# A decoder layer with 32 experts: the order in which the weight queue brings gate/up and down weights

## What is computed

```python
h = xb @ w_gu[e] + b_gu[e]               # 1024 -> 2048
g = jnp.minimum(h[:, 0::2], SWIGLU_LIMIT)
up = jnp.clip(h[:, 1::2], -SWIGLU_LIMIT, SWIGLU_LIMIT)
act = (up + 1.0) * (g * jax.nn.sigmoid(SWIGLU_ALPHA * g))
return act @ w_dn[e] + b_dn[e]           # 1024 -> 1024
```

## Time and profile before

| | us |
|---|---|
| Median of 3 runs | 1151.42 (1150.93 to 1152.32) |
| The profiled execution | 1153.59 |
| Its span | 1151.7 |
| TensorE busy in the span | 1069.7 |
| VectorE busy | 335.8 |
| ScalarE busy | 140.0 |

### The profile page before, as it was taken

One profiled execution on the slowest core, in us unless ns is written; L12 is line 12 of the kernel. 1 busy time (PEld: TensorE's weight loads), 2 busy tenths in 40 slices (PEclk: granted clock), 3 DMA queues, 4 the chain that ended last, 5 costly groups with the idle time before them and its releaser, 6 DMA issues.

```text
span 1151.7 us, 14763 instructions
## 1 busy us (share of the span) xinstructions
PE 1069.7 (93%) x5498; PEld 439.4 (38%) x5498; DVE 335.8 (29%) x728; ACT 140.0 (12%) x264; POOL 20.5 (2%) x45
## 2 busy tenths in 40 slices
PE   3978888999999999999999899999998999999997
PEld 2866344333333333333333333333333333333332
DVE  2386448321212122222222212122121212121213
ACT  2227221000000000000000000000000000000000
POOL 5000000000000000000000000000000000000000
PEclk9998896999999998999999999999999999999999
DMA  8923217999999999999999999999999999999991
GB/s 254 377 100 69 99 48 291 405 417 418 418 420 418 420 418 420 418 418 418 419 417 419 417 419 417 420 417 420 416 420 417 419 419 418 420 418 420 415 415 53
DMA packets 83021, 422.10 MB, mean 367 GB/s; under 512 B 7458, under 2 KB 14906, under 8 KB 50215
## 3 DMA queue, kind: packets, MB, share of 16 engines
q1 hardware_dynamic: 81326, 418.25, 89.7%
q0 software_dynamic: 1232, 2.73, 0.8%
q10 hardware_dynamic: 440, 0.83, 0.2%
HBM read 420.46 MB, written 2.33 MB: 367 GB/s over the span
## 4 chain that ended last, share of the span: by engine, by line
PE 60%; DMA 22%; SPq 8%; DVE 4%; ACT 3%; issue 2%; DVEq 0%; ACTq 0%
PE ps L1451 22%; DMA ring<-in_w_gate_up_dram 20%; PE ps L1492 14%; SPq L273 8%; PE ps L1414 5%; PE ps L1378 4%; PE ps L1140 3%; PE ps L1273 3%; DMA regA<-in_w_in_dram 2%; PE ps L1460 2%; PE ps L1114 2%; PE ps L1389 1%; PE ps L1383 1%; ACT regA L608 1%; PE ps L1422 1%
## 5 line engine op out<-in xcount | busy, mean ns | idle before, releaser
L1451 PE MATMUL ps<-ring,regA 128*64 128x512 f32 x2048 | 461.2, 600 | 24.3 <-DMA ring<-in_w_gate_up_dram 22.4
L1451 PEld LDWEIGHTS ps<-ring,regA 128*64 128x64 f32 x2048 | 145.0, 138 | 334.5 <-issue 259.4
L1060 DVE TENSOR_SCALAR regA<-ps 128x512 f32<-128x512 f32 x32 | 22.1, 692 | 427.1 <-PE ps L1460 427.1
L617 ACT ACTIVATE regA<-regA 128x512 f32<-128x512 f32 x32 | 20.1, 630 | 798.9 <-DVE regA L1060 798.9
L1492 PE MATMUL ps<-ring,regA 128*64 128x512 f32 x512 | 113.4, 595 | 0.0
L1077 DVE COPY regA<-ps 64x512 f32<-64x512 f32 x62 | 42.7, 689 | 222.0 <-PE ps L1492 221.0
L1378 PE MATMUL ps<-regA 128*64 128x256 f32 x512 | 64.1, 393 | 0.0
L1045 DVE TENSOR_TENSOR x_row<-x_row,ps 128x512 f32<-128x512 f32 x72 | 46.1, 684 | 58.8 <-PE ps L1414 58.1
L1492 PEld LDWEIGHTS ps<-ring,regA 128*64 128x64 f32 x512 | 36.4, 137 | 65.8 <-issue 65.6
L1414 PE MATMUL ps<-regA 128*128 128x512 f32 (+1 forms) x136 | 59.7, 594 | 1.1 <-DVE regA L1074 1.1
L1140 PE MATMUL ps<-hT_t,regA 128*128 128x264 f32 x224 | 53.5, 399 | 3.7 <-DMA regA<-in_w_in_dram 3.7
(11 more groups left out here) (270 smaller groups left out, 635.8 us busy)
## 6 DMA issues: line engine op xcount, KB each, us to landing
ring<-in_w_gate_up_dram SPq DMA_DIRECT2D x256, 1024.0 KB, 20.7
ring<-in_w_down_dram SPq DMA_DIRECT2D x64, 1024.0 KB, 22.5
regA<-in_w_down_dram SPq DMA_DIRECT2D x16, 1024.0 KB, 19.4
regC<-in_w_down_dram SPq DMA_DIRECT2D x16, 1024.0 KB, 20.2
regD<-in_w_down_dram SPq DMA_DIRECT2D x16, 1024.0 KB, 21.0
hT_t<-in_w_down_dram SPq DMA_DIRECT2D x16, 1024.0 KB, 21.8
regA<-in_w_in_dram SPq DMA_DIRECT2D x7, 1024.0 KB, 12.1
regA<-in_w_out_dram SPq DMA_DIRECT2D x2, 1024.0 KB, 9.8
```

Source lines behind the costliest of these rows:

```text
L1451: mm = pe.matmul(ps[64 * h:64 * h + 64, 1 + n, :], xT[:, kt % 4, 64 * (kt // 4):64 * (kt // 4) + 64], ring[:, kt, 1024 * h + 512 * n:1024 ...
```

## The change

SP's order stays as it is up to gu(10), dn(11). Then gu(11), gu(12) and dn(12) follow, and from there on an expert's down weights stand behind its own gate/up weights: gu(13), dn(13), ... gu(28), dn(28), gu(29), dn(29). The end is gu(30), gu(31), dn(30), dn(31). The conditions in `load_gu` and `load_dn` are the same.

```diff
+E_TURN = 5
...
-            with sp.Fori(0, E // 2 - 2) as p:
+            with sp.Fori(0, E_TURN) as p:
                 load_gu(p * 2 + 1, p * 2 + 1)
                 load_dn(p * 2 + 2, p * 2 + 2, False)
                 load_gu(p * 2 + 2, p * 2 + 2)
                 load_dn(p * 2 + 3, p * 2 + 3, True)
+            load_gu(2 * E_TURN + 1, 2 * E_TURN + 1)
+            load_gu(2 * E_TURN + 2, 2 * E_TURN + 2)
+            load_dn(2 * E_TURN + 2, 2 * E_TURN + 2, False)
+            with sp.Fori(E_TURN + 1, E // 2 - 2) as p:
+                load_gu(p * 2 + 1, p * 2 + 1)
+                load_dn(p * 2 + 1, p * 2 + 1, True)
+                load_gu(p * 2 + 2, p * 2 + 2)
+                load_dn(p * 2 + 2, p * 2 + 2, False)
             load_gu(E - 3, E - 3)
-            load_dn(E - 2, E - 2, False)
+            load_dn(E - 3, E - 3, True)
             load_gu(E - 2, E - 2)
             load_gu(E - 1, E - 1)
+            load_dn(E - 2, E - 2, False)
             load_dn(E - 1, E - 1, True)
```

TensorE and VectorE run the last two items in another order. The loops over pairs end one pair earlier, item 29 is written out, and `item` is split into functions (`gate_up`, `act_transposes`, `down` on TensorE; `swiglu`, `y_copy` on VectorE) of which the last two items are put together, first TensorE's part, then VectorE's:

```diff
+            def last_two():
+                gate_up(E - 2, True, E // 2)
+                pe.wait_ge(m_idx, E - 1)
+                gather(E - 1, whole)
+                pe.wait_ge(m_act, E - 1)
+                act_transposes()
+                x_transposes(E - 1)
+                gate_up(E - 1, False, E // 2)
+                down(E - 2, True, E // 2)
+                pe.wait_ge(m_act, E)
+                act_transposes()
+                pe.wait_ge(m_idx, E)
+                place(E - 2, beside_last)
+                down(E - 1, False, E // 2)
+                pe.wait_ge(m_add, (N_PLACED - 2) * ADDS + ADDS)
```

```diff
+            def last_two():
+                dve.wait_ge(m_xg, E - 1)
+                choose_rows(E - 1)
+                choose_gates(E - 1)
+                swiglu(E - 2)
+                place_gates(E - 2, upper)
+                dve.wait_ge(m_gated, E - 1)
+                slots_of(E - 1, whole)
+                swiglu(E - 1)
+                dve.wait_ge(m_used, SLOTS * (E - 1) + KT)
+                y_copy(E - 2, upper)
+                add(N_PLACED - 2, beside_last)
+                place_gates(E - 1, whole)
+                dve.wait_ge(m_used, SLOTS * E)
+                y_copy(E - 1, whole)
+                dve.wait_ge(m_gated, E)
+                dve.wait_ge(m_add, (N_PLACED - 2) * ADDS + ADDS)
```

More of the change, by code:

```diff
@@ L1052, in item @@
             def item(q, ahead, r, n_placed):
-                gu = ps[:, 1:3, :].rearrange("p n c -> p (n c)")
                 if ahead:
@@ L1058, in item, with swiglu @@
                     choose_gates(q + 1)
+                swiglu(q)
+                if n_placed is not None:
+                    add(n_placed, beside_ahead if ahead else beside_last)
+                place_gates(q, r)
+                dve.wait_ge(m_used, SLOTS * q + SLOTS)
+                y_copy(q, r)
+                dve.wait_ge(m_gated, q + 1)
+                if ahead:
+                    slots_of(q + 1, upper if r == lower else whole)
+                if n_placed is not None:
+                    dve.wait_ge(m_add, n_placed * ADDS + ADDS)
+            def swiglu(q):
+                gu = ps[:, 1:3, :].rearrange("p n c -> p (n c)")
                 dve.wait_ge(m_gu, q + 1)
@@ L1068, in item, with y_copy @@
                 dve.tensor_tensor(act_sb, up_sb, sig_sb, ALU.mult).then_inc(m_act, 1)
[L1069 to L1072, removed]
+            def y_copy(q, r):
                 if r == whole:
@@ L1077, in item @@
                         dve.tensor_copy(y_sb[n][r, :], ps[64 * n:64 * n + 64, 4, :]).then_inc(m_ysb, 1)
[L1078 to L1083, removed]
             slots_of(0, upper)
@@ L1095, in _ @@
             dve.wait_ge(m_add, ADDS * half + ADDS)
-            with dve.Fori(half, E // 2 - 1) as p:
+            with dve.Fori(half, E // 2 - 2) as p:
                 item(p * 2 + 1, True, lower, p + 1)
                 item(p * 2 + 2, True, upper, None)
-            item(E - 1, False, whole, N_PLACED - 2)
+            item(E - 3, True, lower, N_PLACED - 3)
+            def last_two():
[15 more added lines that the diff above has]
+                dve.wait_ge(m_add, (N_PLACED - 2) * ADDS + ADDS)
+            last_two()
             n_over = dve.value_load(ovi[0:1, 0:1], min_val=0, max_val=N_OVER)
@@ L1440, in place_biases, with item, transposes_copied, gate_up @@
                 mm.then_inc(m_pl, 1)
-            def item(q, ahead, even, n_placed, alone, n_loads):
+            def item(q, ahead, even, n_placed, n_loads):
+                gate_up(q, even, n_loads)
+                if ahead:
+                    pe.wait_ge(m_idx, q + 1)
+                    gather(q + 1, whole if even else upper)
+                pe.wait_ge(m_act, q + 1)
+                act_transposes()
+                def transposes_copied():
+                    pe.wait_ge(m_aT, q + 1)
+                    pe.wait_ge(m_xT, q + 2)
+                if ahead:
+                    x_transposes(q + 1)
+                    if n_placed is not None:
+                        place(q - 1, beside_ahead, False, transposes_copied)
+                down(q, even, n_loads)
+                if n_placed is not None:
+                    pe.wait_ge(m_add, n_placed * ADDS + ADDS)
+            def gate_up(q, even, n_loads):
                 pe.wait_ge(m_xT, q + 1)
@@ L1463, in item, with act_transposes @@
                 mm.then_inc(m_gu, 1)
[L1464 to L1471, removed]
+            def act_transposes():
                 for j in range(4):
@@ L1474, in item, with down @@
                 mm.then_inc(m_atr, 1)
[L1476 to L1483, removed]
+            def down(q, even, n_loads):
                 pe.wait_ge(m_aT, q + 1)
@@ L1495, in item @@
                     mm.then_inc(m_used, 1)
-                if n_placed is not None:
-                    pe.wait_ge(m_add, n_placed * ADDS + ADDS)
             pe.wait_ge(s_xns, 16 * 3)
@@ L1507, in pairs @@
                 with pe.Fori(p0, p1) as p:
-                    item(p * 2 + 1, True, False, p + biases if biases else p, False, p + 1)
-                    item(p * 2 + 2, True, True, None, False, p + 2)
+                    item(p * 2 + 1, True, False, p + biases if biases else p, p + 1)
+                    item(p * 2 + 2, True, True, None, p + 2)
             pe.wait_ge(s_zero, 10)
             half = (E_BIAS - 1) // 2
-            item(0, True, True, None, False, 1)
+            item(0, True, True, None, 1)
             pairs(0, half, 0)
@@ L1516, in _ @@
             pe.wait_ge(m_add, ADDS * half + ADDS)
-            pairs(half, E // 2 - 1, 1)
-            item(E - 1, False, False, N_PLACED - 2, False, E // 2)
+            pairs(half, E // 2 - 2, 1)
+            item(E - 3, True, False, N_PLACED - 3, E // 2 - 1)
+            def last_two():
[8 more added lines that the diff above has]
+                pe.wait_ge(m_act, E)
+                act_transposes()
+                pe.wait_ge(m_idx, E)
+                place(E - 2, beside_last)
+                down(E - 1, False, E // 2)
+                pe.wait_ge(m_add, (N_PLACED - 2) * ADDS + ADDS)
+            last_two()
             pe.wait_ge(S["ovd"], 1)
@@ L1525, in _ @@
                     x_transposes(m + E)
-                    item(m + E, False, True, m + (N_PLACED - 1), True, m + (E // 2 + 1))
+                    gate_up(m + E, True, m + (E // 2 + 1))
+                    pe.wait_ge(m_idx, m + (E + 1))
+                    place(m + (E - 1), beside_last, True, lambda: pe.wait_ge(m_act, m + (E + 1)))
+                    pe.wait_ge(m_act, m + (E + 1))
+                    act_transposes()
+                    down(m + E, True, m + (E // 2 + 1))
+                    pe.wait_ge(m_add, (m + (N_PLACED - 1)) * ADDS + ADDS)
             place(n_over + (E - 1), beside_last, True)
```

## The result

The changed kernel takes 1145.97 us (median of 5 runs, 1145.39 to 1147.4) against 1151.42 for the kernel before (5 runs, 1150.93 to 1153.17): the medians lie 5.4 us apart. The ratio of the runs is 0.9944, 95% interval 0.9932 to 0.9956; of 1151.42 us that is 6.4 us, by the interval 5.1 to 7.8. The sum had said 7.2 us and 1144.2. Its medians lie 7.8 us apart.

The account below looks back on a forecast made before the run. The weight queue was taken to set the pace from expert 13, TensorE's remaining work the end; gate/ups landing 10.35 us earlier bring down(31) from 1142.85 to 1135.6, so 1151.42 − 7.2 = 1144.2 us, range 1140.8 to 1149.0.

Parts of the forecast that it names:

- The sum: Whole kernel: down(31) ends at 1135.6 in place of 1142.85, 7.2 us off the median 1151.42, giving 1144.2 us; chance 0.68.
- The pace: Expert loop from expert 13: the weight queue sets the pace at 60.70 us a pair; TensorE needs 56.68.
- T: End of the weight queue: the landing of the last weights, dn31[3], forecast to stay at 1130.5 us.
- four downs' worth of time: Queue from gu(12) on: every gate/up slot lands four down slots, 10.35 us, earlier, gu29[7] at 1060.2.
- The turn: Queue where its order switches, gu(12) and gu(13): 7.5 and 7.6 us of work still queued at issue, so no loss.
- Both dry-queue rivals: Queue empties: once at the turn, 4.8 us later, 1149.0 (chance 0.08); or again and again, 1158.6 (chance 0.06).
- After the turn: Experts 13 to 19: TensorE, at most 10.5 us behind, is back on the queue's pace by expert 19.
- the rate of 4 us a pair: Expert loop: TensorE's spare time per two experts, 60.70 − 56.68, with which it catches up with earlier landings.
- The rival that saw no effect: After the turn: TensorE stays behind and reads gu(29) at 1070.55 as before; 1152.8 us; chance 0.06.
- The tail: Last experts: gu(30) from 1078.5, gu(31) from 1098.8, place(30) from 1124.2, down(31) to 1135.6, then 8.85 us of unchanged code.
- the difference taken from the median: Final sum: the 7.2 us is subtracted from the runs' median 1151.42, not the profiled 1153.59, giving 1144.2.
- The clock: Rival in the tail: the granted clock falls as down(30) waits slot by slot and place(30) for a copy; chance 0.10.

Follow-up runs that it names:

- c2: Changed kernel's queue with dn(30) back ahead of gu(31), TensorE and VectorE running the old program; ratio 0.9933 to the kernel before.
- c3: Kernel before with only the order of the last two experts on TensorE and VectorE changed, queue order as before; ratio 1.0026, 3.0 us slower.
- d2: Changed kernel with the queue's turn at the very start (E_TURN = 0, first loop taken out); ratio 0.9983 to the kernel before, 2.0 us faster.
- c4: Changed kernel with the queue's turn at gu(27) instead of gu(11); ratio 0.9976 to the kernel before, 2.8 us faster.
- d4: Changed kernel with the queue's turn at gu(21) (E_TURN = 10); ratio 0.9938 to the kernel before.
- c1: The changed kernel timed again without edit, in a second set on one chip; ratio 0.9938 to the kernel before, 7.1 us of 1152.03.
- d3: Changed kernel without placing and adding experts 29 and 30 (results missing), expert 31's down in PSUM bank 2; ratio 0.9902 to the kernel before.

## Why the prediction was right

**The pace and T.** "If the last landing stays at T = 1130.5": it landed at 1129.8, with the front 0.14 us earlier. That four downs' worth of time, 10.35 us, moves from ahead of the gate/ups to behind them held for gu29[7] (1060.2 forecast, 1059.71 measured). With the tail's old order c2 gives the same gain, and with the queue's old order c3 gives none: the earlier landings are the cause.

**The turn.** The backlog of 7.5 and 7.6 us that I had worked out from landings was 7.3 and 7.4, and cost nothing. Both dry-queue rivals rested mainly on these two numbers, and d2 shows that the mechanism is real and what it costs with less. Their price of 4.8 us a restart is no constant: by GB/s the first spell in d2 cost (112 + 133) / 418 × 10 = 5.9 us, near the 3.5 us in which nothing was queued plus the 4.7 − 2.49 = 2.2 by which a landing from an empty queue takes longer than a step of a full one. In the second, with 3.2 us queued, 1.3 us of transfers were missing.

**After the turn.** TensorE was to be back on the queue's pace by expert 19: gu(18) still runs through without a wait at 714.89 and gu19[7] waits for its landing at 754.07. c4 and d4 test the rate of 4 us a pair on which this rests. The rival that saw no effect, with TensorE staying behind, is what c4 shows in part.

**The tail**, forecast and profile: gu(30) from 1078.5, 1078.08; gu(31) from 1098.8, 1098.24; dn30[3]'s read from 1120.7, 1119.99; place(30) from 1124.2, 1123.48; down(31) to 1135.6, 1134.76. Every step came 0.4 to 0.8 us early; T itself was 0.7 early.

**The size.** The step that the first set put in doubt was the difference taken from the median: 1144.2 against 1145.97. The term itself, down(31) ending 7.2 us earlier, measured 8.1 between two profiles whose fronts are 0.14 us apart; c1 gave 7.1 by its ratio and 7.8 by its medians, and both intervals hold 7.2. In the first set the two longest of the five runs of the changed kernel (1147.11 and 1147.4) show a mean granted clock of 0.974, the other three 0.977 or 0.978; without their traces, where they lost time stays open.

**The clock.** I put this rival in the wrong place. In down(30)'s waits and before place(30) the clock stayed at 1.00. It fell to 0.50 at the start of gu(31), in the profiles of c1, c3, c4, d2, d3 and d4 (not in the first one), where `last_two` lets TensorE wait for the copy of expert 31's inputs, and there it cost 1.9 us. In c3 and c4 this went straight into the time. In c1 it went into the wait for dn30[3]: gu(31) took 15.47 us and down(31) still ended 75.13 us after gu29[7]'s read. A fall like the one at gu(9) of the kernel before, where the clock stood at 0.58 ahead of 16.88 us of gate/up against the usual 13.73, would have cost 3.15 us. That waits between the last matmuls bring the clock down is not borne out for down(30): its waits of some 0.6 us a slot (0.9 in the forecast) left it at 1.00.

**What I had not seen:** half of the change brings nothing that these runs can tell. The prediction costed the queue and the new tail together and never asked what the old tail would do behind the new queue. c2 answers it: the same time within the intervals, with a dozen lines of SP's program and nothing else.

Whether a tail could reach d3's floor with all its work was not tried. In front of down(31) stand 1.0 us of TensorE's wait for the copies of expert 30's results (they end at 1121.97 + 1.41 = 1123.38, place(30) starts at 1123.48) and 4.2 of place(30); without them, part of that time would be waits for the last slots, so that 3 us of it are to be had at most, about the scatter of these runs.

## What to carry to other kernels

Where a queue that is always full feeds an engine with little time to spare, the order of the queue does not change when the last byte lands as long as the queue stays full (here 1129.8 against 1130.5), but it decides how much work is left then: bring last what has the least work behind it, here down weights. An engine that lags needs about as many rounds as lead divided by gain per round (10.35 / 4, so three; one gave a part of the gain) to use earlier landings, so reorder at least that long before the end. And before a load is put behind one that waits for a slot, work out from issue and landing times how many microseconds the queue still holds at that moment: here 7.3 us were enough, with 3.2 us queued 1.3 us of transfers were lost, and with an empty queue 5.9.

## What the runs showed of the hardware

The mean granted clock and the count of matmul instructions, in the profile of the kernel before:

```profile
core 0: 1151.7 us, clock 0.977
...
L1451 PE MATMUL ps<-ring,regA 128*64 128x512 f32 x2048 | 461.2, 600 | 24.3 <-DMA ring<-in_w_gate_up_dram 22.4
```

The program calls the float32 matmul of L1451 four times a slot, 32 × 8 × 4 = 1024 times in all; the trace has 2048 instructions for it, two for each call.

The granted clock fell after a very short idle stretch. In c4, in order of time, and by stretches of it:

```profile
1101.30 4.92 PE L1506 MATMUL ps<-ring,regA 128*64 128x512 f32 x14 [0.69 <-ACT regA L617]
...
1100.00:1101.00 1.00, 0.61 (x4) 0.37 (x4) 0.00 (x0) 0.78 (x2) 0.00 (x0) 1.00 1.09 459
1101.00:1103.00 2.00, 1.70 (x6) 0.69 (x8) 0.00 (x0) 0.24 (x1) 0.00 (x0) 0.68 0.98 410
1103.00:1105.00 2.00, 2.00 (x6) 0.49 (x4) 0.00 (x0) 0.00 (x0) 0.00 (x0) 0.50 1.01 414
```

TensorE stood for 0.69 us, after the gather's small matmuls and eight transposes, and its granted clock was 0.68 from 1101 to 1103 and 0.50 from 1103 to 1105. The waits of up to 1.4 us between full gate/up slots left it at 1.00, so the length of the wait alone does not decide. In the first profile of the changed kernel the same wait of 0.69 us, at 1098.24, left the clock at 1.00. What decides it was not tested.

The last landing came well after most of the bytes. At the end of the changed kernel's queue, whose last slot landed at 1129.8 (columns of the earlier trace rows):

```profile
1120.00:1124.00 4.00, 3.03 (x14) 1.20 (x15) 1.38 (x2) 0.60 (x1) 0.00 (x0) 1.00 0.79 323
...
1128.00:1130.00 2.00, 2.00 (x12) 0.72 (x10) 1.15 (x3) 0.00 (x0) 0.00 (x0) 1.00 0.04 16
```

From 1124 on the mean busy share of the 16 DMA engines was 0.16 and less, and 0.23 MB were moved until 1130 (61, 37 and 16 GB/s, for 2 us each), of slots of 1 MB. A backlog worked out from landings can thus be longer than what most of the engines still have to do. d2's second spell, where 1.3 us of transfers were missing with 3.2 us queued by the landings, fits that; by how much it is too long was not measured.
